# Expert weights of a mixture-of-experts step fetched as eight rows of one matrix per piece, instead of four rows of two

## What is computed

```python
pg_top, g_idx = lax.top_k(pg, 1)
le = le.reshape(n, N_GROUPS, EXPERTS_PER_GROUP)[jnp.arange(n), g_idx[:, 0]]
pe_top, e_idx = lax.top_k(softmax(le), TOP_K_IN_GROUP)
hid = jax.nn.silu(jnp.einsum('nd,edf->nef', x, w_gate)) * jnp.einsum('nd,edf->nef', x, w_up)
y = jnp.einsum('nef,efd->nd', hid * gate[..., None], w_down)
```

## Time and profile before

| what | value |
|---|---|
| median of three runs | 2065.97 us |
| the profiled execution | 2063.22 us |
| its span, first to last instruction | 2061.3 us |
| PE busy | 1812.5 us, 88% |
| DVE busy | 1174.2 us, 57% |
| ACT busy | 906.3 us, 44% |
| read from HBM | 432.44 MB |
| issues of `w_gate` and `w_up`, median size | 128 each, 512 KB |
| issues of `w_down` | 64, 1024 KB |
| products of L2121, 16 per expert | 512, so the overflow branch did not run |

### The profile page before, as it was taken

The page is one execution under the profiler, slowest core; times in us unless marked ns, Lnnn a source line. Parts: engine busy times, 40 slices in busy tenths (PEclk is TensorE's granted clock), DMA queues, the critical chain, the costliest instruction groups (busy, mean ns, idle before and its releaser), DMA issues.

```text
span 2061.3 us, 32450 instructions
## 1 busy us (share of the span) xinstructions
PE 1812.5 (88%) x12399; PEld 1614.1 (78%) x12399; DVE 1174.2 (57%) x1201; ACT 906.3 (44%) x976; POOL 267.1 (13%) x256
## 2 busy tenths in 40 slices
PE   3999778989879999899999998974599999999991
PEld 3999658978669999899999998974476666666661
DVE  4342434547654465633344444336498888888875
ACT  3332013225343333333343333331488888887872
POOL 1000110010250000000000000001244324223230
PEclk8999799989989999999999999995799999999995
DMA  6554637430466545255555555452499999999974
GB/s 196 163 163 151 214 102 250 155 123 1 147 155 205 163 132 167 90 168 164 163 163 164 163 164 188 155 191 106 157 390 397 381 382 377 382 381 383 385 290 163
DMA packets 230555, 434.77 MB, mean 211 GB/s; under 512 B 18656, under 2 KB 174896, under 8 KB 219184
## 3 DMA queue, kind: packets, MB, share of 16 engines
q1 hardware_dynamic: 205792, 372.28, 51.9%
q0 software_dynamic: 16688, 47.08, 7.6%
q10 hardware_dynamic: 8000, 14.36, 2.2%
HBM read 432.44 MB, written 33.59 MB: 226 GB/s over the span
## 4 chain that ended last, share of the span: by engine, by line
PE 62%; DMA 20%; DVE 9%; ACT 5%; issue 3%; SPq 1%; POOL 1%; POOLq 0%; ACTq 0%; DVEq 0%
DMA mem<-in_w_up 16%; PE ps L1777 16%; PE ps L1778 16%; PE ps L1779 16%; DVE split L1540 4%; ACT split L976 3%; PE ps L1827 2%; PE ps L1872 1%; PE ps L1727 1%; PE ps L1762 1%; PE ps L1886 1%; DMA mem<-ypair_d 1%; PE ps L2121 1%; PE ps L1797 1%; PE ps L2089 1%
## 5 line engine op out<-in xcount | busy, mean ns | idle before, releaser
L1540 DVE TENSOR_TENSOR split<-mem,split 128x2048 fp32r<-128x2048 f32 x192 | 437.1, 2289 | 65.9 <-ACT split L976 63.8
L976 ACT CAST split<-mem 128x2048 fp32r<-128x2048 f32 x192 | 364.9, 1911 | 95.1 <-DMA mem<-in_w_up 44.9
L1146 DVE TENSOR_TENSOR ring_lo<-mem,ring_hi 128x2048 fp32r<-128x2048 f32 x78 | 178.4, 2291 | 235.3 <-ACT ring_hi L742 234.0
L1779 PE MATMUL ps<-h_hi,ring_lo 128*128 128x288 f32 x1024 | 304.5, 297 | 0.0
L742 ACT CAST ring_hi<-mem 128x2048 fp32r<-128x2048 f32 x78 | 148.4, 1907 | 340.8 <-DMA mem<-in_w_in 263.1
L1779 PE MATMUL ps<-u_lo,ring_lo 128*128 128x288 f32 x896 | 267.3, 298 | 0.0
L2121 PE MATMUL ps<-split,xgT 128*128 128x512 f32 x512 | 208.7, 408 | 13.8 <-DVE xgT L1641 13.5
L2122 PE MATMUL ps<-split,xgT 128*128 128x512 f32 x512 | 201.7, 394 | 0.0
L1779 PEld LDWEIGHTS ps<-h_hi,ring_lo 128*128 128x128 f32 x1024 | 195.1, 191 | 0.0
L1777 PE MATMUL ps<-u_lo,ring_hi 128*128 128x288 f32 x608 | 184.6, 304 | 11.5 <-DVE ring_lo L1146 11.5
L1779 PEld LDWEIGHTS ps<-u_lo,ring_lo 128*128 128x128 f32 x896 | 171.1, 191 | 0.0
(11 more groups left out here) (370 smaller groups left out, 3871.8 us busy)
## 6 DMA issues: line engine op xcount, KB each, us to landing
mem<-in_w_in SPq DMA_DIRECT2D x104, 1024.0 KB, 5.2
mem<-in_w_gate SPq DMA_DIRECT2D x128, 512.0 KB, 6.1
mem<-in_w_up SPq DMA_DIRECT2D x128, 512.0 KB, 11.9
mem<-in_w_down SPq DMA_DIRECT2D x64, 1024.0 KB, 12.7
mem<-in_w_pa SPq DMA_DIRECT2D x16, 1024.0 KB, 5.4
mem<-in_w_pb SPq DMA_DIRECT2D x16, 1024.0 KB, 5.4
mem<-in_w_o SPq DMA_DIRECT2D x16, 1024.0 KB, 5.4
xt<-in_cache_k_cmp POOLq DMA_DIRECT2D x16, 256.0 KB, 3.6
```

What stands on the lines that cost most here:

```text
L976: nc.scalar.copy(split[slot][:, 0], staging[q]).then_inc(done, 1)
L1146: ins = V.tensor_tensor(ring_lo[:, u, k], ring[:, u, k], hi[:].bitcast(F32), ALU.subtract)
L1540: V.tensor_tensor(split[slot][:, 1], staging[q], split[slot][:, 0].bitcast(F32), ALU.subtract).then_inc(done, 1)
L1779: ins = M(out, ring_lo[:, u, k, cols], hi[:, x, :], start=False, stop=(x == KT - 1))
```

## The change

Pieces 0 to 3 hold eight rows of one matrix: q = 0 and 2 take `w_gate`, q = 1 and 3 `w_up`, rows 0 to 7 of a partition's sixteen in the first two and 8 to 15 in the others. Each is one DMA of 1 MB, 128 runs of 8 KB. Two neighbouring split slots form a pair, and a product takes its 256 gate columns from the first and its 256 up columns from the second, 16 KB apart. `gate_up` waits for both pieces of a pair, makes 16 products, and the last counts `piece_used` up by two. The semaphore counts follow. The overflow branch (L1055, L2178), for experts with over 64 tokens, changes likewise.

```diff
--- before.py
+++ after.py
@@ -239,7 +239,8 @@
         xg = mem[0:CAP, X0:X0 + D]
         g_ffn = mem[:, X0:X0 + D]
         SP0 = K0
-        split = [rounded(f"split{n}", [P, 2, PIECE], SP0 + 2 * PIECE * n) for n in range(4)]
+        pairs = [rounded(f"pair{n}", [P, 2, 2, PIECE], SP0 + 4 * PIECE * n) for n in range(2)]
+        split = [pairs[n // 2][:, n % 2] for n in range(4)]
         y_sb = mem[:, SP0 + 8 * PIECE:SP0 + 8 * PIECE + D // 2]
         halves = mem[:, SP0 + 8 * PIECE + D // 2:SP0 + 8 * PIECE + D // 2 + 2 * ED]
         assert X0 + D <= SP0 and SP0 + 8 * PIECE + D <= END
@@ -487,9 +488,8 @@
 
             def load_piece(e, q, done):
                 if q < 4:
-                    for c, view in enumerate((wg, wu)):
-                        sp.dma_start(staging[q][:, c * 4 * ED:(c + 1) * 4 * ED],
-                                     view[:, ds(e, 1), 4 * q:4 * q + 4].rearrange("p a k f -> p (a k f)")).then_inc(done, 16)
+                    half = 8 * (q // 2)
+                    sp.dma_start(staging[q], (wg, wu)[q % 2][:, ds(e, 1), half:half + 8].rearrange("p a k f -> p (a k f)")).then_inc(done, 16)
                 else:
                     sp.dma_start(staging[q], wd[:, ds(e, 1), q - 4].rearrange("p a f -> p (a f)")).then_inc(done, 16)
 
@@ -977,8 +977,8 @@
 
 
             act.wait_ge(s.w_used, 4 * IT_END)
-            round_weights(0, 0, piece_sems[0], 32, s.hi_done)
-            round_weights(1, 1, piece_sems[1], 32, s.hi_done)
+            round_weights(0, 0, piece_sems[0], 16, s.hi_done)
+            round_weights(1, 1, piece_sems[1], 16, s.hi_done)
             for t in range(3):
                 act.wait_ge(s.normed, 3 + t + 1)
                 act.dma_start(h2_d[t * P:t * P + ROWS[t], :], hn_at[1][t][0:ROWS[t]]).then_inc(s.h2_out, 16)
@@ -998,7 +998,7 @@
                     return
                 n = before(e, q)
                 act.wait_ge(s.piece_used, n - 3)
-                round_weights((6 * b + q) % 4, q, piece_sems[q], (e + 2) * 32 if q < 4 else (e + 1) * 16, s.hi_done)
+                round_weights((6 * b + q) % 4, q, piece_sems[q], (e + 2) * 16 if q < 4 else (e + 1) * 16, s.hi_done)
 
             def rows_hi(b, full, n, done):
                 act.wait_ge(full, n)
@@ -1020,8 +1020,8 @@
 
             act.wait_ge(s.h2_out, 48)
             act.wait_ge(s.lg_full, 3)
-            round_weights(2, 2, piece_sems[2], 32, s.hi_done)
-            round_weights(3, 3, piece_sems[3], 32, s.hi_done)
+            round_weights(2, 2, piece_sems[2], 16, s.hi_done)
+            round_weights(3, 3, piece_sems[3], 16, s.hi_done)
             rows_hi(0, s.xt_done, 1, s.xgh_done)
             piece_hi(0, 0, 0)
             piece_hi(0, 0, 1)
@@ -1058,7 +1058,7 @@
                     for q in range(6):
                         if q >= 4:
                             act.wait_ge(s.o_used, o * 6 + (q - 3))
-                        round_weights(q % 4, q, s.o_w, (o + 1) * 160, s.o_hi)
+                        round_weights(q % 4, q, s.o_w, (o + 1) * 96, s.o_hi)
                     halves_left(2, s.o_used, o * 6 + 4, s.fold_in)
                     act.wait_ge(s.fold_done, o + (NE + 1))
                     A(hgate, ps[0:CAP, 2, 0:ED], ACT.Silu).then_inc(s.o_hg, 1)
@@ -2111,16 +2111,17 @@
                     ins = T(ps[:, k // 8, (k % 8) * CAP:(k % 8 + 1) * CAP], xg[:, k * P:(k + 1) * P], ident[0:CAP, 0:CAP])
                 ins.then_inc(done, 1)
 
-            def gate_up(x, bank, slot0, lo, n, done, pieces=range(4)):
+            def gate_up(x, bank, slot0, lo, n, done, halves=range(2)):
 
                 out = ps[:, bank].rearrange("p (c f) -> p c f", c=2)
-                for q in pieces:
-                    pe.wait_ge(lo, n + (q + 1))
-                    w = split[(slot0 + q) % 4].rearrange("p h (c k f) -> p h k c f", c=2, k=4)
-                    for k in range(4):
-                        M(out, x[:, 4 * q + k].rearrange("p h c -> p (h c)"), w[:, 0, k], start=(q == 0 and k == 0), stop=False)
-                        ins = M(out, x[:, 4 * q + k].rearrange("p h c -> p (h c)"), w[:, 1, k], start=False, stop=(q == 3 and k == 3))
-                    ins.then_inc(done, 1)
+                for half in halves:
+                    pe.wait_ge(lo, n + (2 * half + 2))
+                    w = pairs[(slot0 // 2 + half) % 2][:].rearrange("p c h (k f) -> p h k c f", k=8)
+                    for k in range(8):
+                        both = x[:, 8 * half + k].rearrange("p h c -> p (h c)")
+                        M(out, both, w[:, 0, k], start=(half == 0 and k == 0), stop=False)
+                        ins = M(out, both, w[:, 1, k], start=False, stop=(half == 1 and k == 7))
+                    ins.then_inc(done, 2)
 
             def fold(bank, ready, n, done):
 
@@ -2160,11 +2161,11 @@
                     fold(2 + b, s.fold_in, e + 1, s.fold_done)
                     if not last:
                         pe.wait_ge(s.xgT_ready, e + 2)
-                        gate_up(xgT[1 - b], 3 - b, 6 * b, s.lo_done, before(e, 0), s.piece_used, range(2))
+                        gate_up(xgT[1 - b], 3 - b, 6 * b, s.lo_done, before(e, 0), s.piece_used, range(1))
                     apart(pe, s.hid_done, e + 1, s.pe_passed)
                     hid_T(2 + b, s.ht_done)
                     if not last:
-                        gate_up(xgT[1 - b], 3 - b, 6 * b, s.lo_done, before(e, 0), s.piece_used, range(2, 4))
+                        gate_up(xgT[1 - b], 3 - b, 6 * b, s.lo_done, before(e, 0), s.piece_used, range(1, 2))
                     if not (isinstance(e, int) and e >= NE - 2):
 
                         apart(pe, s.xg_in, (e + 3) * 16, s.pe_passed)
```

## The result

The changed kernel takes 2053.47 us (median of 10 runs, 2047.99 to 2062.9) against 2065.36 us for the kernel before in the same session (10 runs, 2060.37 to 2082.46): a ratio of 0.9943, 95% interval 0.9917 to 0.9968. Its profiled execution took 2054.53 us, with a span of 2052.8 us; for the kernel before these were 2063.22 and 2061.3. The difference is 8.7 us in the profiled executions and 11.9 us in the medians.

What follows compares the result with a forecast made beforehand. The DMA engines were taken as the bound at 17.27 us an expert. Saving 9.6 us over 30 experts, less 1 us for gather bursts, brings expert 30 8.6 us earlier: 2057.4 us against the 2065.97 median, range 2049 to 2067.

Steps and rivals of the forecast that it cites:

- The two lines: Paths to expert 30's L1664: DMA engines reach it at 1986.5, engines' loop at 1983.1; the later sets the end.
- The engines' loop: From L1664 through PE, ACT and DVE back to L1664: 16.65 us an item with releases by pair, up from 15.9.
- the release from product to ACT: Handover in the engines' loop from the last product of half 1 on PE to ACT: 0.43 us.
- The DMA pace: Weight loads on the DMA engines: from 17.27 to 16.95 us per expert.
- One sign that was named: Starts of L1664 on DVE would lie 16.9 to 17.0 us apart if the forecast was right.
- The loads: Gate and up loads in 8 KB runs: 36 packets fewer per engine save 0.32 us an expert, 9.6 us over 30.
- the upper end of 0.46: Largest saving per expert on the weight loads, from a fixed packet cost of 12.7 ns: 0.46 us.
- a constant rate: Assumption for the DMA packets: fixed cost of 10.3 to 12.7 ns each, the bytes beside it at one unchanging rate.
- the slow rival: Gate and up products slow down from runs 16 KB apart: at 0.06 us each, 2081.7 us; chance 0.13.
- the second rival: Release by pairs replaces the DMA as bound: loop closes at 17.0 us, time 2063.5 us; chance 0.18.
- PE's waits for a pair: PE in gate_up waits for two pieces where it waited for one: costs nothing at either half.
- Bytes, not packets: Bytes fill the DMA engines: 0.17 us an expert gained gives 2060.9 us, nothing gained 2066; chance 0.16.

Runs made afterwards that it cites:

- light loads: Kernel before and changed kernel, each fetching only half the rows of each gate or up piece from expert 1 on: 2036.39 and 2060.1 us.
- the run whose shorter loop leaves the loads to bind: Changed kernel with rows_T before hid_T and its wait on PE, rows_hi and rows_lo behind piece 5 on ACT and DVE: 2057.7 us, ratio 0.9960.
- the repeat: The changed kernel run unaltered once more in a later session: 2054.30 us, ratio 0.9960 to the kernel before.
- the two DMAs by rows: Changed kernel with each gate and up piece fetched in two DMAs of four rows, 4 KB packets, all 128 partitions: 2066.92 us, ratio 1.0017.

## Why the prediction was right, step by step

**The two lines.** The engines' loop was put at 16.65 us and measured 16.72 us; of its terms only the release from product to ACT was off (0.50 for 0.43). That the loop is a line of its own, and not a late effect of the loads, is shown by the run of after with light loads (16.7 throughout) beside that of before (15.9). The DMA pace was put at 16.95: by the stage's rates, 17.27 x 383 / 390 = 16.96 us with the 390 GB/s of the run whose shorter loop leaves the loads to bind; 16.87 and 17.00 with the 392 and 389 of the two runs of after (383: the queue view of before for the same 455 us). Expert 30 was forecast at 1987.5 and came at 1986.81, the profiled execution at 2054.6 and came at 2054.53. So close an agreement is partly luck: the repeat needed 4.0 us more for the same 30 items. One sign that was named did not show: L1664 at 16.9 to 17.0 us. The items took 16.79 us on average (16.92 in the repeat), 16.72 up to expert 21; only the last nine show the loads. The sign did not follow from the sum either, which has 1987.5 - 1483.55 us for 30 items, 16.80 each. The median lies 3.9 us under the 2057.4 given, since the profiled execution of before lay 2.75 us under its median, and that of after 1.1 us over it.

**The loads.** 0.32 us an item was taken. In time that passes, 17.27 less 16.87 to 17.00 is 0.27 to 0.40, which holds it. In engine time, with its overlaps, the main queue went from 42.0 us a MB to 40.6 (40.9 in the repeat), 0.44 to 0.55 us an item, near or over the upper end of 0.46. The packet durations give the price that was meant: 9 ns for each of 36 packets, 0.32 us. That this is the term to the hundredth is luck, since 0.32 was the middle between 0.17 and 0.46 and the price of 10.3 to 12.7 ns comes from 4 KB packets of 162.9 ns on average, not 159. What failed in part is "a constant rate" beside the packet's own cost: the slow packets differ from form to form, as the 8 KB packets by odd and even partitions and the 4 KB runs in one DMA show. For the change itself this made little difference: its DMAs cover the 128 partitions with one run each, as do those of w_down, from which the price was read.

**The rest.** The products with runs 16 KB apart cost nothing (they start 0.235 us apart, 0.237 before), so the slow rival falls; no run shows the 0.05 us that bounded it. For two thirds of the items the release took over from the DMA, as the second rival had it, but at 16.72 us and not at 17.0; PE's waits for a pair don't show. "Bytes, not packets" falls by the runs of 2 and 4 KB, with the same bytes and 44.4 and 42.5 us a MB, and by the two DMAs by rows with 41.9.

## What to carry to other kernels

When a change makes transfers cheaper and releases coarser, write down both paces, the transfers' and the engines' own loop; the later one sets the end, and loads made light in an experiment show the engines' pace directly. Lengthen a run while keeping one DMA over all partitions in order: longer packets from a DMA over every other partition brought nothing here. An operation moved out of a loop on one engine can stand in the same loop on another, as rows_T did. And before a difference is called the cost of a packet, look at the packets that nothing holds up: their most frequent duration gave the same 9 ns at both steps where the totals gave 8 to 24.

## What the runs showed of the hardware

With gate and up in DMAs that reach only the lower or only the upper 64 partitions, the rate of the stage falls from 392 to 222 GB/s, although the queue holds both halves, the packets have 8 KB and the DMA share is 1.00. Nearly all 8 KB packets were slow, w_down's too: the median is 588 ns, against 311 and 309 ns in the two runs of after. The table by stage of that run, columns as above:

```profile
1525.00:1980.00 455.00, 307.16 (x1147) 214.75 (x1147) 233.38 (x136) 214.15 (x166) 59.91 (x60) 0.82 1.00 222
```

A full DMA share is therefore no sign that the DMA engines move what they can. The granted clock fell as well, to a mean of 0.82 of the upper level, 2.4 GHz, where PE was busy 307 of 455 us; in after it was 433 us at 1.00.

The Trainium skill, "SBUF — State Buffer", section "Door 1: The DMA port swizzle (why [64,N] ≈ [32,N])", says that partitions 0 to 63 reach only 8 of 16 ports, with about 218 GB/s as the asymptote. The 222 GB/s of this trace are near that, but a third of its weights are w_down's over 128 partitions, so the rate of the halves by themselves isn't shown. By that section's map the odd or the even partitions reach all 16, and that form ran at 381 GB/s, far from half, but not at 392.

Why it stayed at 381, and why 4 KB runs with gaps in one DMA took 42.5 us a MB where two DMAs of 4 KB took 41.9, was not settled: the order of the partitions that are written, the engine that gets each row and the order in which memory is read all change together in these forms. The Trainium skill, "DMA: Bandwidth & Descriptors", section "The descriptor swizzle", says that in a transfer over 128 partitions each engine writes one port, and leaves other shapes open. That would leave room for engines that meet at a port in the odd and even form, but gives no reason for the form with gaps, which covers 128 partitions; no run here shows which engine wrote which partition.
